# Expert rows from group 1 on read their tokens from two PSUM banks, with four banks for jobs and at most seven gathers in flight

## The reference

```python
idx = ...                      # 128 expert numbers for each token, by two top-k steps
gate = jax.nn.softmax(best, axis=-1)
u = u_tab[idx]
h = jax.nn.gelu(jnp.einsum('bthkd,btd->bthk', u, xi), approximate=False)
w = gate * h
return jnp.einsum('bthk,bthkd->btd', w, v_tab[idx])
```

## Time and profile before

| | us |
|---|---|
| median of 3 runs (2821.18, 2822.25, 2834.01) | 2822.25 |
| the profiled execution | 2821.56 |
| its span | 2819.7 |
| POOL busy, 1059 instructions | 1146.2 |
| DVE busy, of it 512 row sums | 1138.8, 616.7 |
| PE busy, of it the rows at L1529 | 2067.9, 1024.1 |

### The profile page before, as it was taken

How to read it: one execution, slowest core, us unless ns; L and a number is a source line. 1 busy time by engine, 2 the same in 40 slices (tenths; PEclk the granted TensorE clock), 3 DMA queues, 4 the chain that set the end, 5 groups by cost and what they waited for, 6 DMA issues and landing times.

```text
span 2819.7 us, 20906 instructions
## 1 busy us (share of the span) xinstructions
PE 2067.9 (73%) x7424; PEld 1067.1 (38%) x7424; DVE 1138.8 (40%) x2587; ACT 427.5 (15%) x1103; POOL 1146.2 (41%) x1059
## 2 busy tenths in 40 slices
PE   4624799766989866988766767778999986546564
PEld 2422345222535322535322222227867853212221
DVE  2367655875253894344794544431112031000001
ACT  1201231111131111131101111111022101000000
POOL 0004656777565777665677777750000000000000
PEclk8666999989999989999889999998986987878787
DMA  5126999989999999999999999986750566999996
GB/s 186 52 72 227 389 333 374 378 312 364 399 366 348 384 330 355 396 376 329 362 339 375 354 349 363 379 299 140 159 119 9 157 252 279 427 427 427 427 426 271
DMA packets 229052, 867.90 MB, mean 308 GB/s; under 512 B 23360, under 2 KB 26048, under 8 KB 216656
## 3 DMA queue, kind: packets, MB, share of 16 engines
q0 software_dynamic: 147456, 536.94, 50.7%
q1 hardware_dynamic: 81488, 329.56, 32.0%
HBM read 865.37 MB, written 1.05 MB: 307 GB/s over the span
## 4 chain that ended last, share of the span: by engine, by line
PE 40%; DVE 20%; DMA 17%; POOL 9%; issue 7%; another core or an unknown queue 3%; ACT 3%; SPq 1%; DVEq 0%; ACTq 0%
PE psum L1430 11%; PE psum L1529 11%; PE psum L1422 8%; DVE rows L812 6%; DMA rows<-in_peer_v,idx 5%; POOL rows L569 5%; POOL rows L560 5%; DMA rows<-in_w_e_gate 4%; DMA rows<-in_w_e_down 4%; DMA rows<-in_w_e_up 3%; PE psum L1685 3%; PE psum L1411 2%; DVE work L743 2%; DVE work L742 1%
## 5 line engine op out<-in xcount | busy, mean ns | idle before, releaser
L1529 PE MATMUL psum<-rows,diag 128*128 128x512 f32 x2048 | 1024.1, 642 | 332.2 <-DMA rows<-in_peer_v,idx 129.1
L560 POOL DMA_INDIRECT rows<-in_peer_u,idx x512 | 576.8, 1127 | 496.2 <-DVEq L594 231.3
L812 DVE CUSTOM_DVE_ANT_0 rows<-rows,px 128x1024 f32<-128x1024 f32 x512 | 616.7, 1226 | 333.2 <-DMA rows<-in_peer_u,idx 300.5
L1529 PEld LDWEIGHTS psum<-rows,diag 128*128 128x128 f32 x2048 | 390.1, 202 | 915.9 <-issue 624.3
L569 POOL DMA_INDIRECT rows<-in_peer_v,idx x512 | 565.6, 1105 | 243.7 <-issue 132.3
L1430 PE MATMUL psum<-work,ring 128*128 128x256 f32 (+1 forms) x1664 | 284.9, 334 | 0.7 <-ACT work L1115 0.7
L1430 PEld LDWEIGHTS psum<-work,ring 128*128 128x128 f32 x1664 | 260.3, 193 | 29.9 <-issue 5.2
L1224 ACT ACTIVATE diag<-ident,wgt 128x128 f32<-128x128 f32 x512 | 178.0, 392 | 555.8 <-DVE wgt L820 206.1
L1422 PE MATMUL psum<-ring,work 128*128 128x512 f32 (+1 forms) x452 | 206.3, 612 | 7.6 <-ACT work L1115 3.8
L1115 ACT ACTIVATE work<-psum 128x512 f32<-128x512 f32 (+5 forms) x167 | 85.5, 522 | 635.7 <-PE psum L1422 200.7
L1057 DVE TENSOR_TENSOR work<-kept,psum 128x512 f32<-128x512 f32 x8 | 8.2, 1030 | 427.7 <-PE psum L1685 427.7
(11 more groups left out here) (269 smaller groups left out, 1446.6 us busy)
## 6 DMA issues: line engine op xcount, KB each, us to landing
ring<-in_w_in SPq DMA_DIRECT2D x16, 2048.0 KB
rows<-in_w_e_gate SPq DMA_DIRECT2D x16, 2048.0 KB, 21.9
rows<-in_w_e_up SPq DMA_DIRECT2D x16, 2048.0 KB, 20.3
rows<-in_w_e_down SPq DMA_DIRECT2D x16, 2048.0 KB, 21.1
ring<-in_gla_w_in SPq DMA_DIRECT2D x12, 2048.0 KB
ring<-in_w_e_gate SPq DMA_DIRECT2D x12, 2048.0 KB, 19.6
ring<-in_w_e_up SPq DMA_DIRECT2D x12, 2048.0 KB, 19.5
ring<-in_w_e_down SPq DMA_DIRECT2D x12, 2048.0 KB, 20.0
```

The lines of the kernel that those rows point to most:

```text
L560: pool.indirect_dma_start(out=u_rows[:, n % RU, :], out_offset=None, in_=a["peer_u"][g // 2], in_offset=bass.IndirectOffsetOnAxis(ap=idx[: ...
L812: V_.tensor_tensor_reduce(out=u, in0=u, in1=px[:, g % 2, :], scale=1.0, scalar=0.0, op0=ALU.mult, op1=ALU.add, accum_out=hid[:, r:r + 1]). ...
L1529: last = mm(psum[:, 6 + c, :], diag[:, n % DIAGS, :], v_rows[:, n % RV, c * BANK:(c + 1) * BANK], start=r == 0, stop=r == P - 1)
```

## The change

From group 1 on the row sums take their tokens from PSUM banks 4 and 5. ACT copies them there from `px` at the start of each group, after DVE's last row sum of the group before (`u_used` >= n), and DVE's first row sum of the group waits for the copy (`x_ready`). Jobs are given banks by a table, `job_banks`: six banks up to group 0's stages, four (0 to 3) beside groups 1 to 3, eight in `mix` and `moe`; PE waits for the eviction of the last job that had the bank. On POOL, `landed` makes a gather wait until the one 7 before it has landed: each of the first 12 u gathers, and then once per pair, at the v gather, for the one 6 before it, so that with the following u gather seven are in flight.

```diff
--- before.py
+++ after.py
@@ -32,8 +32,8 @@
 DIAGS, LEAD = 6, 2
 BLK, LAG = 8, 12
 AHEAD = LAG
+FLIGHT = 7
 NU = 4 * P
-NB = 6
 
 
 
@@ -152,6 +152,21 @@
 
 
 ROW_TARGET = row_targets()
+
+
+def job_banks():
+
+    bank, same, at, last = [], [], 0, {}
+    for key, _ in [(key, name) for key in STAGES for name in stage_jobs(*key)]:
+        n = 6 if key in BEFORE or key in BESIDE[0] else 8 if key in AFTER else 4
+        at = (at + 1) % n
+        bank.append(at)
+        same.append(last.get(at, 0))
+        last[at] = len(bank)
+    return bank, same
+
+
+JOB_BANK, BANK_FREE = job_banks()
 
 
 class Rows:
@@ -261,6 +276,10 @@
         diag = sb("diag", [P, DIAGS, P])
 
         psum = ctx.enter_context(nc.psum_tensor("psum", [P, 8, BANK], f32))
+
+        def x_now(g):
+
+            return psum[:, 4:6, :].rearrange("p a b -> p (a b)") if g else px[:, 0, :]
 
         def carve(region, at, *shape):
             n = int(np.prod(shape))
@@ -367,6 +386,7 @@
         u_here = [sem(f"u_here{i}") for i in range(RU)]
         v_here = [sem(f"v_here{i}") for i in range(RV)]
         u_used = sem("u_used")
+        x_ready = sem("x_ready")
         v_used = sem("v_used")
         gelu_ready = sem("gelu_ready")
         wgt_ready = sem("wgt_ready")
@@ -399,7 +419,7 @@
             return [4 * (g // 2) + g % 2, 4 * (g // 2) + g % 2 + 2]
 
         def job_bank(key, name):
-            return psum[:, (JOB[key + (name,)] - 1) % NB, :]
+            return psum[:, JOB_BANK[JOB[key + (name,)] - 1], :]
 
 
         def piece_source(what, c0, n):
@@ -561,6 +581,15 @@
                                         in_offset=bass.IndirectOffsetOnAxis(ap=idx[:, g % 2, r:r + 1], axis=0)
                                         ).then_inc(u_here[n % RU], 16)
 
+            gathers = [at for n in range(NU + AHEAD)
+                       for at in ([(u_here, RU, n)] if n < NU else []) + ([(v_here, RV, n - AHEAD)] if n >= AHEAD else [])]
+
+            def landed(k):
+
+                if k >= 0:
+                    here, slots, n = gathers[k]
+                    pool.wait_ge(here[n % slots], 16 * (n // slots + 1))
+
             def fetch_v(n):
                 g, r = n // P, n % P
                 if n >= RV:
@@ -570,11 +599,17 @@
                                         in_offset=bass.IndirectOffsetOnAxis(ap=idx[:, g % 2, r:r + 1], axis=0)
                                         ).then_inc(v_here[n % RV], 16)
 
+            k = 0
             for n in range(NU + AHEAD):
                 if n < NU:
+                    if n < AHEAD:
+                        landed(k - FLIGHT)
                     fetch_u(n)
+                    k += 1
                 if n >= AHEAD:
+                    landed(k - FLIGHT + (n < NU))
                     fetch_v(n - AHEAD)
+                    k += 1
 
             pool.wait_ge(emptied, JOB[("mix", 0, "O1_7")])
             pool.iota(e_iota, [[1, S]], base=0, channel_multiplier=0, allow_small_or_imprecise_dtypes=True).then_inc(e_iota_ready, 1)
@@ -808,8 +843,10 @@
                 if n < NU:
                     g, r = n // P, n % P
                     dve.wait_ge(u_here[n % RU], 16 * (n // RU + 1))
+                    if r == 0 and g:
+                        dve.wait_ge(x_ready, g)
                     u = u_rows[:, n % RU, :]
-                    V_.tensor_tensor_reduce(out=u, in0=u, in1=px[:, g % 2, :], scale=1.0, scalar=0.0, op0=ALU.mult,
+                    V_.tensor_tensor_reduce(out=u, in0=u, in1=x_now(g), scale=1.0, scalar=0.0, op0=ALU.mult,
                                             op1=ALU.add, accum_out=hid[:, r:r + 1]).then_inc(u_used, 1)
                 n -= LAG - LEAD - BLK
                 if n >= BLK and n % BLK == 0 and n <= NU:
@@ -1209,6 +1246,11 @@
 
             def row(n):
 
+                if n % P == 0 and P <= n < NU:
+
+                    act.wait_ge(dve_step, STEP["dve"][("route", n // P, "xn")])
+                    act.wait_ge(u_used, n)
+                    A_.activation(x_now(n // P), px[:, n // P % 2, :], ACT.Copy).then_inc(x_ready, 1)
                 if n >= BLK and n % BLK == 0 and n <= NU:
                     r = (n - BLK) % P
                     c = slice(r, r + BLK)
@@ -1385,9 +1427,9 @@
 
             def open_bank(key, name):
                 n = JOB[key + (name,)]
-                if n > NB:
-
-                    pe.wait_ge(emptied, n - NB)
+                if BANK_FREE[n - 1]:
+
+                    pe.wait_ge(emptied, BANK_FREE[n - 1])
                 return job_bank(key, name)
 
             def close(key, name, last):

```

## The result

The changed kernel is slower by 0.6%: 2838.1 us (median of 20 executions, 2827.0 to 2851.3) against 2821.0 us for the kernel before on the same chip (20 executions, 2801.6 to 2834.9), a ratio of 1.0062 with a 95% interval of 1.0044 to 1.0079. The forecast was 2760 us, faster by 2.2%, with a range from 2735 to 2805 us. The profiled execution took 2843.5 us.

What follows compares the result with a forecast made beforehand. The prediction took POOL, its gathers held up by DVE's row sums, to underfeed the DMA queue. Gains of 30 and 36 us less 3 us for copies made 63 us off, so 2760 us, range 2735 to 2805.

Steps and rivals of the forecast that it cites:

- the two-operand instructions of route and gla: Groups 1 and 2: these DVE instructions still hold up gathers after the change, an estimated 12 us of excess a group.
- the copies: ACT's copy of x at the start of groups 1 to 3: costs 1 us a group, 3 us, bounds 0 to 6.
- the banks: Four PSUM banks for jobs beside groups 1 to 3: no cost, since evictions come at once.
- rival 2: Nothing happens, because gathers stay held or the DMA engines are already full: 2822 us +- 5, chance 0.07.
- 65 ns by the estimate: Row sums reading PSUM: possible extra time each, which would put the time some 6 us above the forecast.
- The gain is between 28 and 41 us: Last group: row sums from PSUM no longer hold up gathers; 30 us taken as the gain.
- the books: POOL's time in the last group: 327.9 us of undisturbed gathers, 38.0 us excess busy, 12.8 us excess idle, together 378.7 us.
- rival 1: PE's release of v slots becomes late at full DMA pace: 2807 us, milder forms down to 2785, chance 0.16.
- 18 us for each of groups 1 and 2: Groups 1 and 2: gain from gathers no longer held by row sums, 36 us for two, bounds 8 and 33 a group.
- 54 us of stops: Last group, if full pace causes late releases: a 4 us stop for every 25 us at full pace.
- At most seven in flight: POOL's v gathers wait for an earlier landing: no cost taken, bound 10 us in all.
- Two of its own tests: Profile signs: POOL's idle growth over half its busy loss would mean wrong; last group's DMA rate was expected near 400 GB/s.

Runs made afterwards that it cites:

- e2_cap_only: The kernel before with only the limit of seven gathers in flight added, in a set without late releases: ratio 1.0053 to the kernel before.
- e3_banks_only: The kernel before with only the new table of banks, row sums still reading SBUF, no limit, without late releases: ratio 0.9998 to the kernel before.
- e10_no_cap_second: The changed kernel without the limit on gathers in flight, in a set with late releases: ratio 1.0028 to the kernel before.
- e1: The changed kernel without the limit on gathers in flight, in a set without late releases: ratio 0.985 to the kernel before.
- e8_psum_last_no_cap: The changed kernel without the limit, tokens in PSUM for the last group only, with late releases: ratio 0.9987 to the kernel before.
- e12_copy_hidden: The changed kernel without the limit, first four row sums of groups 1 to 3 reading SBUF, with late releases: ratio 1.0038 to the kernel before.
- e9: The changed kernel itself, measured again in a set with late releases: ratio 1.0077 to the kernel before.
- set 1: The first follow-up runs, trying the change's parts one by one on one chip without late releases; the kernel before took 2745 us there.
- e6_cap9: The changed kernel with at most nine gathers in flight instead of seven, with late releases: ratio 1.0077 to the kernel before.

## Why the prediction was wrong

**Right: what bounds POOL, and what PSUM does to it.** Held gathers are gone from the last group, and in groups 1 and 2 some 10 us each are left, as the prediction had it for the two-operand instructions of route and gla; in groups 1 to 3 the busy time above 0.937 us per gather fell from 129.7 to 21.3 us. `e2_cap_only` shows that such time can cost its full length (29.7 us held, the last group 17.6 us longer than with 12.2 us). The row sums take 1220 ns, the copies 1.0 us, the banks nothing (`e3_banks_only`, without late releases), mix and moe didn't move (921.1 and 920.2 us from the last expert row on). The Trainium skill's rule ("SBUF — State Buffer", § Who interferes with whom), that a VectorE instruction with two SBUF inputs contends with a GpSimd instruction that reads SBUF, was used against rival 2. The trace agrees: with one operand of the row sums in PSUM, the last group's gathers take 937 ns in the mean. The 120 cycles that the Trainium skill gives VectorE for a PSUM source against 58 for an SBUF source ("VectorE: DVE Perf Modes", § The TRN2 errata), worth 65 ns by the estimate, are not seen: 1220 ns against 1224.

**Wrong: "The gain is between 28 and 41 us; a part of what is saved will reappear as waits for slots, and I take 30 us" for the last group.** It is 1.5 us in the changed kernel, 5 us with the limit out of the way (378.2 to 373.0, from different sets), and 1.4 us in the set without late releases (339.0 to 337.6). The sum took the 38.0 us held away and left the 12.8 us waited as they were. With the row sums in PSUM and no limit the books read 0.8 us held and 45.2 us waited (`e10_no_cap_second`): 50.8 us became 46.0. A v gather may not go before PE's release of its slot, and while it waits for that, it doesn't matter how long the gathers ahead of it took. Whether the same late releases were there before, in the shadow of the held time, or whether the freed queue brought more of them, these runs don't separate; the counts under rival 1 speak for some of the second.

**Wrong: 18 us for each of groups 1 and 2.** Here lies most of the miss: these groups became 11.0 and 11.4 us longer, where 36 us less were forecast. Without late releases the profiled executions give 12.4 and 9.4 us (`e1` against `e3`), about two thirds of the term, and the medians 38.7 us for the whole change without its limit, of 63. With late releases they give nothing or a loss: 436.7 and 435.5 us in `e10_no_cap_second` against 428.2 and 438.2 with SBUF reading and the limit in the same set, and 426.8 and 429.2 in `e8_psum_last_no_cap`, of another set, which reads SBUF there. Why they get longer, and not only stay, is open. The gap at the border isn't it (`e12_copy_hidden`). One road is visible and wasn't tried by itself: the gelu stands behind waiting diagonals in ACT's queue, and DVE's waits for it in groups 1 and 2 are 52.4 us in `before`, 77.5 in `e10_no_cap_second` and 52.5 in `e1_no_cap`.

**Rival 1 was the case, and was priced too low.** It described the row of 1631 us rightly (ACT and POOL released together, late, by one PE row), got 0.16, and was booked as the gain of the last group and half of the rest lost, 2807 us, though the prediction's own 54 us of stops were "more than the gain there". Slower than before was in its price nowhere. The argument against it, that the excess idle time of the last stretch was only 12.8 us, was the error: idle time on POOL measures late releases only where POOL is otherwise free, and before it was held for 38.0 us. By the trace of before, of 116 rows of the last group 38 had neither diagonal nor v gather released within 8 us of the row's end; in `after` it is 50, in `e10_no_cap_second` 61. Not all of these were waited for: without late releases the count is 14 in `e3_banks_only` and 2 in `e1_no_cap`.

**Wrong: "At most seven in flight: I take 0; the bound is 10 us".** On top of PSUM reading it cost 15 us (`e9` against `e10`), 16.5 us by itself in set 1 (2761.9 against 2745.4), and nothing by itself with late releases. The prediction asked whether a gather issued 7.7 us earlier has landed, and took 6.5 us from issue to use from the kernel before, whose POOL is held. Once POOL is free the queue grows: in the last group of `e1_no_cap` a gather takes 12.7 us from issue to its last part (6.6 in `e3_banks_only`), and 9.7 are in flight on average and up to 14 (5.1 and 6). The 8.5 and 12 in the expectation of `e6_cap9` don't count to the last part, for which the limit waits. So the limit binds there where it would not have before. Over all groups of `e2_cap_only` POOL waits 108.4 us for landings, 76 times, and none of it in the last group; the prediction's bound of 10 us had a few tenths for each of some 40 gathers in a group. That it costs by taking away a backlog that a pause could be bridged with is argued; with SBUF reading its cost in the last group is held time (`e2_cap_only`), and with late releases the landings aren't recorded. Nine was no better than seven, and I can't say where the cost ends.

**The sum, as measured.** With late releases: PSUM reading +7 us (2827.1 against 2820.1), the limit on top +15, together +22 in that set and +17 in the first comparison, instead of -63. Two of its own tests fired: POOL's idle time before gathers grew by 134.7 us (739.9 to 874.6) where its busy time lost 110.3, and the last group went at 366 GB/s, not near 400.

No version beat the kernel before in both kinds of sets. PSUM reading without the limit is 1.5% faster in one and 0.3% slower in the other.

## What to carry to other kernels

When an engine is held up and also waits for slots, don't subtract the one and leave the other: ask how long the release it would wait for next has been due, and from what moment on it could have gone. A stop that the trace can't explain (here two engines released together, long after the row they wait for) is a bound of its own, and belongs into the forecast at full price. And a limit in flight is to be judged by how long a landing takes once the queue is free, and not by how long it took before; compare kernels within one set only, and repeat the comparison on another before believing a cause.

## What was not expected of the hardware

- PE's releases reach ACT and POOL up to 16 us after the recorded end of the row (13.6 and 14.3 us in the place shown), while PE goes on at its pace, and DVE's releases come within 0.5 us in `before`, `after` and `e10_no_cap_second`. TensorE's clock doesn't make this stop: the granted clock around that place is at its full level, 2.4 GHz (PE, PEld, DVE, ACT, POOL busy, PE clock, DMA share, GB/s):

```profile
1620.00:1630.00 10.00, 7.19 (x16) 2.52 (x15) 4.70 (x8) 0.57 (x2) 7.48 (x9) 1.00 1.02 409
1630.00:1640.00 10.00, 7.37 (x16) 2.47 (x15) 4.99 (x9) 1.40 (x4) 5.09 (x6) 1.00 0.97 363
1640.00:1650.00 10.00, 6.54 (x14) 2.28 (x14) 3.69 (x6) 1.01 (x3) 7.48 (x8) 1.00 0.97 356
```

- Whether this happens belongs to the set and not to the kernel: four comparisons had it (before at 2806 to 2821 us), two did not (2743 and 2745 us). It moves the kernel before by 2.2 to 2.9% and goes with the sign of this change. Its cause stays open. In the packets something else differs: in the last group 1.0 to 1.4% of the 4 KB packets take over 0.5 us (`before`, `after`, `e10_no_cap_second`), and none in `e1_no_cap`. The granted clock in groups 1 and 2 is lower too, 0.90 and 0.91 in `e10_no_cap_second` against 0.96 and 0.95 in `e1_no_cap`, while before and after the groups it agrees (0.70, and 0.83 or 0.84); whether that follows the pauses of PE or adds to them wasn't tried.
- With half of PE's row products left out, the granted clock of the last group is 0.59 on average, between its two levels of 1.2 and 2.4 GHz, against 1.00 in `e1_no_cap` (columns as above), one record of a product of 512 columns lasts 1057 ns in the median of the run, where it is 592 in `after` and `e1_no_cap`, and the group takes 336.5 us all the same:

```profile
1415.00:1750.00 335.00, 252.91 (x271) 62.72 (x270) 159.74 (x274) 48.71 (x152) 244.63 (x262) 0.59 1.03 409
```
